# Taking the causal mask of the stick-breaking heads out of the score matmuls and into the scan's marks

## What is computed

```python
z = einsum('bqhd,bshd->bhqs', qb, kf) * dh ** -0.5
causal = (spos[None, :] < tpos[:, None])[None, None]
log_beta = jax.nn.log_sigmoid(z)
log_keep = jnp.where(causal, log_beta - z, 0.0)
between = lax.cumsum(log_keep, axis=3, reverse=True) - log_keep
a = jnp.where(causal, jnp.exp(log_beta + between), 0.0)
o = einsum('bhqs,bshd->bqhd', a, vf)
```

## Time and profile before

| | us |
|---|---|
| median of 3 executions | 804.84 (803.2 to 805.67) |
| the profiled execution | 803.94 |
| its span, first to last instruction | 802.2 |
| around the span | 1.74 |
| mean granted TensorE clock | 0.992 of full |

### The profile page before, as it was taken

One profiled execution on the slowest core, in us unless ns is written; L12 is line 12 of the kernel. 1 busy time (PEld: TensorE's weight loads), 2 busy tenths in 40 slices (PEclk: granted clock), 3 DMA queues, 4 the chain that ended last, 5 costly groups with the idle time before them and its releaser, 6 DMA issues.

```text
span 802.2 us, 10493 instructions
## 1 busy us (share of the span) xinstructions
PE 784.3 (98%) x3724; PEld 655.4 (82%) x3724; DVE 390.4 (49%) x536; ACT 351.8 (44%) x519; POOL 417.9 (52%) x248
## 2 busy tenths in 40 slices
PE   8998999999999999999998999999999999999996
PEld 6776888888888888888877988888888888888885
DVE  4669979989657565389237200000000020444464
ACT  6665266766758585632254322221222232232242
POOL 5556455666777878334552234434444444444463
PEclk9999999999999999999999999999999999999999
DMA  8311352311304231223293113322333332223312
GB/s 334 106 47 53 116 163 78 104 53 53 104 10 118 69 108 53 80 80 105 104 302 93 53 53 105 105 80 80 102 105 105 105 100 68 93 105 105 105 54 105
DMA packets 100012, 79.40 MB, mean 99 GB/s; under 512 B 2818, under 2 KB 90890, under 8 KB 99979
## 3 DMA queue, kind: packets, MB, share of 16 engines
q1 hardware_dynamic: 99978, 78.97, 31.1%
HBM read 76.85 MB, written 3.68 MB: 100 GB/s over the span
## 4 chain that ended last, share of the span: by engine, by line
PE 92%; DVE 5%; ACT 2%; issue 0%; DMA 0%; SPq 0%; DVEq 0%; ACTq 0%
PE ps L472 24%; PE ps L451 19%; PE ps L453 19%; PE ps L452 19%; PE ps L684 2%; PE ps L536 2%; PE ps L673 2%; DVE score L1359 2%; PE ps L652 1%; PE ps L654 1%; DVE x L1519 1%; ACT y_buf L823 1%; PE ps L506 0%; DMA g_cols<-in_gain_cols 0%; DVE xg_lo L1300 0%
## 5 line engine op out<-in xcount | busy, mean ns | idle before, releaser
L1119 POOL TENSOR_TENSOR w_lo<-raw,w_hi 128x1024 fp32r<-128x1024 f32 x82 | 198.1, 2417 | 266.7 <-ACT w_hi L794 237.7
L451 PE MATMUL ps<-h_hi,w_hi 128*128 128x512 f32 (+1 forms) x608 | 236.3, 389 | 0.0
L453 PE MATMUL ps<-h_hi,w_lo 128*128 128x512 f32 (+1 forms) x608 | 233.8, 385 | 0.0
L452 PE MATMUL ps<-h_lo,w_hi 128*128 128x512 f32 (+1 forms) x608 | 233.5, 384 | 0.0
L794 ACT ACTIVATE w_hi<-raw 128x1024 fp32r<-128x1024 f32 (+1 forms) x78 | 82.6, 1061 | 292.8 <-PE ps L453 195.4
L453 PEld LDWEIGHTS ps<-h_hi,w_lo 128*128 128x128 f32 x608 | 114.2, 188 | 22.9
L452 PEld LDWEIGHTS ps<-h_lo,w_hi 128*128 128x128 f32 x608 | 114.5, 188 | 21.0
L451 PEld LDWEIGHTS ps<-h_hi,w_hi 128*128 128x128 f32 x608 | 114.4, 188 | 20.7
L1562 DVE TENSOR_TENSOR act<-silu,ps 128x512 f32 (+1 forms) x22 | 15.1, 688 | 211.3 <-PE ps L453 211.3
L1205 POOL TENSOR_TENSOR w_lo<-raw,w_hi 128x1024 fp32r<-128x1024 f32 x30 | 76.9, 2567 | 32.1 <-ACT w_hi L914 31.7
L1567 DVE TENSOR_TENSOR d_lo<-act,d_hi 128x512 fp32r<-128x512 f32 x18 | 43.1, 2396 | 51.7 <-ACT d_hi L1067 51.7
(11 more groups left out here) (195 smaller groups left out, 1335.1 us busy)
## 6 DMA issues: line engine op xcount, KB each, us to landing
raw<-in_w_gate_up SPq DMA_DIRECT2D x44, 512.0 KB, 4.5
raw<-in_w_in SPq DMA_DIRECT2D x40, 512.0 KB, 4.1
raw<-in_w_down SPq DMA_DIRECT2D x22, 512.0 KB, 3.8
xf<-in_first SPq DMA_DIRECT2D x8, 512.0 KB, 6.5
raw<-in_w_out SPq DMA_DIRECT2D x8, 512.0 KB, 3.8
x_in<-in_x SPq DMA_DIRECT2D x4, 512.0 KB, 8.5
raw<-in_w_branch_sb SPq DMA_DIRECT2D x8, 256.0 KB, 2.9
raw<-in_w_branch_sparse SPq DMA_DIRECT2D x8, 256.0 KB, 3.0
```

The costliest lines, as they stand in the source:

```text
L451: mm(acc, whi_c, a_hi_, start=first, stop=False)
L452: mm(acc, whi_c, a_lo_, start=False, stop=False)
L453: return mm(acc, wlo_c, a_hi_, start=False, stop=last)
L1119: nc.gpsimd.tensor_tensor(w_lo[:, at(u), :], raw[:, at((d % 2) * 2 + u), :], w_hi[:, at(u), :], sub).then_inc(w_lo_done, 1)
```

## The change

The three mask matmuls of each stick-breaking head go, with the two constants that they use and the instructions that make these (GpSimd's memset and affine_select of tri_f, VectorE's copy into neg_tri and scaling of the identity into big_ident), and one wait of GpSimd.

The mask moves into the scan: ends is now 1 on the diagonal of each block (four copies of the identity in place of four one-column fills), and the last column of each block of keep_buf and e_buf is set to 0 once, by eight one-column fills on VectorE ahead of the first scan. Run backwards, the product starts at 0, stays 0 behind the diagonal, and becomes 1 on it. The sigmoids must leave these last columns alone, so each of the two activations of 1280 columns becomes four, of 511, 383, 127 and 255 columns. Only the last of four signals.

```diff
             ins = mm(z(0, a, a + n), q_lo[:, h, b * P:(b + 1) * P], k_both[:, h, 0:n], start=False,
-                         stop=i >= HEADS, skip_group_check=True)
-            if i < HEADS:
-                for a, n in ((PACK[4] + 3 * P, 1), (PACK[3] + 2 * P, 2), (PACK[2] + P, 1)):
-                    ins = mm(z(0, a, a + n * P), big_ident[:, :], neg_tri[:, 0:n, :].rearrange("p t n -> p (t n)"),
-                             start=False, stop=True, skip_group_check=True)
+                         stop=True, skip_group_check=True)
...
-            run(keep_buf[:, :], z(0, 0, TRI), ACT.Sigmoid, scale=-1.0).then_inc(keep_done, 1)
+            for b in (3, 2, 0, 1):
+                a, n = PACK[b + 1], (b + 1) * P - 1
+                ins = run(keep_buf[:, a:a + n], z(0, a, a + n), ACT.Sigmoid, scale=-1.0)
+            ins.then_inc(keep_done, 1)
             if i >= 2:
                 sc.wait_ge(probs_turned, i - 1)
-            run(e_buf[:, i % 2, :], z(0, 0, TRI), ACT.Sigmoid).then_inc(beta_done, 1)
+            for b in (3, 2, 0, 1):
+                a, n = PACK[b + 1], (b + 1) * P - 1
+                ins = run(e_buf[:, i % 2, a:a + n], z(0, a, a + n), ACT.Sigmoid)
+            ins.then_inc(beta_done, 1)
...
-        nc.gpsimd.memset(tri_f[:, :, :], -1.0).then_inc(const_gp, 1)
-        gp.wait_ge(const_gp, 3)
-        nc.gpsimd.affine_select(tri_f[:, :, :], tri_f[:, :, :], pattern=[[0, 2], [1, P]], base=0, channel_multiplier=-1,
-                                compare_op=ALU.is_ge, fill=0.0).then_inc(tri_in, 1)
-        gp.wait_ge(tri_in, 1)
+        gp.wait_ge(const_gp, 2)
...
-        ve.wait_ge(tri_in, 1)
-        nc.vector.tensor_copy(neg_tri[:, :, :], tri_f[:, :, :]).then_inc(const_ve, 1)
-        ve.wait_ge(const, 2)
-        ts(big_ident[:, :], ident[:, :], -MASKED, None, ALU.mult).then_inc(const_ve, 1)
-
...
+        ve.wait_ge(const, 2)
         for b in range(TB):
-            last = PACK[b + 1] + (b + 1) * P - 1
-            ins = nc.vector.memset(ends[:, last:last + 1], 1.0)
+            own = PACK[b + 1] + b * P
+            ins = nc.vector.tensor_copy(ends[:, own:own + P], ident[:, :])
         ins.then_inc(ends_done, 1)
...
+        for b in range(TB):
+            last = PACK[b + 1] + (b + 1) * P - 1
+            nc.vector.memset(e_buf[:, :, last:last + 1], 0.0)
+            ins = nc.vector.memset(keep_buf[:, last:last + 1], 0.0)
+        ins.then_inc(edges_done, 1)
+        ve.wait_ge(edges_done, 1)
         ve.wait_ge(ends_done, 2)
         kept_after(0)
         break_probs(0)
```

More of the change, by code:

```diff
@@ L147, in build @@
     ident = sb("ident", P)
-    big_ident = sb("big_ident", P, F32R)
-    neg_tri = sb("neg_tri", [2, P], F32R)
     rel_in_rows = sb("rel_in_rows", HEADS, rows=BUCKETS)
@@ L204, in build @@
     relu_buf = sb("relu_buf", [2, TRI])
-    tri_f = sb("tri_f", [2, P])
     f_bias, zeros8 = sb("f_bias", 384, rows=HEADS), sb("zeros8", 384, rows=HEADS)
@@ L271, in build @@
     y_done = sems("y_done0", "y_done1")
-    const, const_gp, const_ve, tri_in = sems("const", "const_gp", "const_ve", "tri_in")
+    const, const_gp, edges_done = sems("const", "const_gp", "edges_done")
     small_turned, far_kept, small_kept, gain_spread = sems("small_turned", "far_kept", "small_kept", "gain_spread")
```

## The result

In the first comparison the changed kernel had a median of 796.64 us (796.3 to 797.23, 4 executions) against 804.02 us (803.18 to 805.67, 4 executions) of the kernel before: a ratio of 0.9909 (95% interval 0.9887 to 0.9932), 7.4 us. The forecast was 802.6 us, with 801.0 to 804.4 as its range.

A forecast was written before the change was run, and what follows sets the result against it. TensorE, busy 98% of the span, was taken to bound the kernel. 2.9 us freed less a 0.6 us stall gives 2.3 us, so 804.84 - 2.3 = 802.6 us, range 801.0 to 804.4.

The forecast's parts named there:

- TensorE frees 0.36 us a head, 2.9 in all: Stick-breaking heads: without mask matmuls TensorE's period between turnings falls from 13.59 to 13.23 us, 2.9 us over eight heads.
- A stall of 0.6 us at the turning of head 1: TensorE, arriving earlier at head 1's turning, waits 0.6 us for VectorE's output sum of head 0; no wait elsewhere.
- ScalarE 0.05 us for each more piece: Sigmoid passes: each added activation costs ScalarE 0.05 us, 0.3 us a head, 2.6 us in all, none on the path.
- VectorE's preparations hidden: Before the first scan: fills, wait and copies take 2.1 of VectorE's 5.36 us idle time, so cost nothing.
- The rival of a second stall at head 5: More stall: 0.95 us at head 1 and 0.8 us at head 5, where VectorE meets GpSimd; 803.7 us, chance 24%.
- that of slower: VectorE waits for GpSimd at the turnings of heads 1 and 5, stalls of 4.3 against 2.9 us; 806.2 us, chance 5%.
- that of less freed: Heads: only 0.29 us a head go and the fill still starts late, gain 1.9 us; 802.9 us, chance 9%.
- The base and the range: Whole kernel: base 804.84 us, medians wandering by about a us, range 801.0 to 804.4 us.
- The difference between the kernels: Whole kernel: 2.9 us freed in the heads less a 0.6 us stall, 2.3 us gained.

The follow-up runs named there:

- e3: Changed kernel with three matmuls of 128, 256 and 128 columns put back per stick-breaking head, into unread PSUM columns: 802.87 us, ratio 1.002 to the kernel before.
- the two further comparisons: Changed kernel, unaltered, run again twice against the kernel before: 801.92 against 803.22 us, ratio 0.9979, and 798.0 against 803.15 us, ratio 0.9953.
- e1: Kernel before with only the 24 mask matmuls left out, constants, buffer places and whole activations kept: 801.42 us, ratio 0.999 to the kernel before.
- e9: Changed kernel, unaltered, run once more against the kernel before: 798.0 against 803.15 us, ratio 0.9953.

## Why the prediction was wrong, point by point

- *TensorE frees 0.36 us a head, 2.9 in all*: right. From head 1 to head 6 the turnings of the changed kernel follow each other at 13.23 to 13.27 us, those of e3 at 13.58 or 13.59. With the stall it makes 2.17 (forecast 2.3), in five profiles without mask matmuls against five with them or their stand-ins.
- *A stall of 0.6 us at the turning of head 1, put down to the output sum, and nowhere else*: right, 0.62 us. The two rests of keys ended 0.5 us behind GpSimd's subtractions again, as the earlier trace rows let expect (128.40 + 1.27 = 129.67 and 130.22 for the first).
- *ScalarE 0.05 us for each more piece*: right, 1.28 us a pass for 1.30. The estimate by the Trainium skill (ScalarE: Activation LUTs, section "What ACT_TABLE_LOAD costs"), 93 ns a piece, would make this pitch 1.14 + 0.28 = 1.42 us, more than the 1.28 of these rows.
- *VectorE's preparations hidden*: right. The fills began at 114.16, 4.8 us ahead of the scan; they took 0.2 us in all where I had put about 1, and VectorE's idle time was 4.67 us (5.36 before; I had expected some 3). The four copies took longer than I said, 1.37 for 1.1 us, since one of them was held up (0.97 for 0.21 us):

```profile
77.14 1.37 DVE L1367 COPY ends<-ident 128x128 f32<-128x128 f32 x4
```

- *The rival of a second stall at head 5, that of slower, and that of less freed*: none came. The profile names no other wait of TensorE between the scores of head 0 and the turning of head 15, and 8 x 0.36 - 0.62 = 2.26 us leaves 0.1 us for any that it doesn't name.
- *The base and the range*: wrong, and this is the failed step. I took 804.84 us, the median of three executions, as the kernel's time, and allowed 0.6 to 0.9 us for what such a median wanders, "as 803.2 to 805.67 show"; and I wrote that behind the heads "TensorE is the chain again, so what was gained stays". The runs show 798.1 to 807.8 us for that kernel, 796.2 to 804.9 for the changed one, and medians of 800.3, 803.2 and 803.2 for some 30 executions each of the kernel before. The three executions that I saw, and the profile with them, all lay in the upper half. Of the 8.2 us between my base and the measured 796.64, the base itself makes 0.8 (804.02 with the fourth execution) and the change 2.2; the other 5.2 are the scatter that I had put at under one. The profile that I read held the sign of it: two additions of 2.88 us beside two of 1.22 in the same loop, a wait of TensorE of 3.2 us in the norms with some 1.1 us of lower clock behind it, and a clock of 0.66 in one window of the start, by estimate up to 5 x 0.34 = 1.7 us. I looked only at the stretch of the change. With these three taken off as what may go, 804.84 - 2.9 - 3.2 - 1.1 - 1.7, the range would have reached down to 796.
- *The difference between the kernels* was right for its reason and not by luck: forecast 2.3 us, 2.17 in the heads, repeated to 0.04 us, and 2.6 between the means of the two further comparisons. Of the 7.4 us of the first, 5.2 come from which executions fell together there.

What stays open: the first comparison had four executions of the changed kernel below 797.3 and four of the kernel before above 803. Of the 24 later executions of the changed kernel 6 lie below 797.3, of the 88 later ones of the kernel before 42 above 803. So four of four is not what independent draws would often give. Whether the chip or the hour favours one outcome, and whether the 2.2 us by which the changed kernel reaches the norms earlier shift the odds there, these runs can't tell, nor what makes the weights land earlier or later; the medians of the kernel before (800.3 beside one set, 803.2 beside two, each set on another chip) suggest that the odds differ between sets. Nor was it tried to remove the start's fall of the clock.

## What to carry to other kernels

Where TensorE is busy throughout, the distance between equal points of its queue, with and without the matmuls in question, gives the worth of leaving them out to 0.1 us, and the next stall is read off as the smallest margin between a producer's end and TensorE's start, less what TensorE gains up to there. Before a change is credited with a difference, cut both traces at fixed points of the critical engine: a gain in a stretch that the change doesn't touch belongs to the execution until a second and third profile repeat it. And an operation that takes 2.9 us here and 1.2 us there in one trace is a race with another engine; the most that it can give or take belongs into the range of every prediction on that kernel, whatever is changed.

## What the runs showed of the hardware

- A VectorE addition with two SBUF inputs waits for a GpSimd subtraction that began before it (2.88 us for 1.22 when GpSimd was 0.59 us ahead, 3.48 us when it was 0.01 us ahead, in e1), and runs at full speed when it began first (1.23 us, GpSimd 0.81 us behind, and 0.17 us behind in e9). The Trainium skill (SBUF — State Buffer, section "SBUF: two separate sides") states this lock, and that the one which starts first has it; the traces agree. I had not expected that when one weight transfer lands decides it, and that there are two ways to lose: too early GpSimd is ahead of the addition, too late its second subtraction is ahead of the scaling. Between the two cases lie 4 to 7 us of the kernel's time (341.2 to 341.8 us against 345.7 to 348.1).
- A wait of TensorE in the norms costs more than itself. Behind the 3.2 us of before the granted clock was 0.51 and 0.64 of full in two windows of 2 us, and from the first to the last of six pairs of matmuls of 512 columns it took 3.49 us (429.07 to 432.56), in the changed kernel 2.37 (421.92 to 424.29). In all six profiles in which TensorE waited 2.67 to 4.25 us before the second turning the clock of the 2 us behind its start was 0.50 to 0.58; in the six in which it waited 0.56 us or less it was 1.00.
- Three matmuls of 128, 256 and 128 columns cost TensorE 0.36 us, the same with an identity and a triangle as with other operands into unused columns (212.81 us in both).
